# Norms with the rounded part first, four weight tiles walked together, and low parts made by VectorE

## The reference

```python
for i in range(DEPTH):                       # DEPTH = 4, kind = i % 3
    mp = mixer(xp)                           # hgrn2, dsa or s5
    xp = layer_norm(DN_ALPHA * xp + mp, ln_mix_g[i], ln_mix_b[i])
    xp = layer_norm(DN_ALPHA * xp + sq_relu_mlp(xp, mlp_w1[i], mlp_w2[i]), ln_ffn_g[i], ln_ffn_b[i])

def layer_norm(x, g, b):
    mu = jnp.mean(xf, -1, keepdims=True)
    var = jnp.mean(jnp.square(xf - mu), -1, keepdims=True)
    return ((xf - mu) * lax.rsqrt(var + LN_EPS) * g + b)
```

## Time and profile before

| what | us |
|---|---|
| timed runs, median (lowest to highest) | 3243.29 (3243.13 to 3245.08) |
| profiled execution, its own time | 3235.7 |
| profiled execution, span from first to last instruction | 3233.9 |
| TensorE busy in the span | 2885.5 |
| VectorE, ScalarE, GpSimd busy | 1479.6, 1051.1, 1042.7 |
| mean granted TensorE clock (share of full) | 0.923 |

### The profile page before, as it was taken

The page is one execution under the profiler, slowest core; times in us unless marked ns, Lnnn a source line. Parts: engine busy times, 40 slices in busy tenths (PEclk is TensorE's granted clock), DMA queues, the critical chain, the costliest instruction groups (busy, mean ns, idle before and its releaser), DMA issues. The chain is left out here.

```text
span 3233.9 us, 54787 instructions
## 1 busy us (share of the span) xinstructions
PE 2885.5 (89%) x22296; PEld 2787.9 (86%) x22296; DVE 1479.6 (46%) x2170; ACT 1051.1 (33%) x1612; POOL 1042.7 (32%) x548
## 2 busy tenths in 40 slices
PE   7999789999899998999943777999989998899997
PEld 7999789999769998999942677999989997799997
DVE  4555363251327425506249844713425554461442
ACT  4554432222331434212241223312235554331222
POOL 2000453445523126344430025534440001453442
PEclk9999899999897979999976579999999998899999
DMA  4222122222334322222231012222223221122221
GB/s 138 81 81 80 55 72 85 91 84 85 104 84 164 123 69 78 85 91 91 85 95 23 23 50 79 85 85 91 85 72 100 90 81 56 60 86 83 91 85 65
DMA packets 118301, 267.52 MB, mean 83 GB/s; under 512 B 10274, under 2 KB 57890, under 8 KB 118018
## 3 DMA queue, kind: packets, MB, share of 16 engines
q1 hardware_dynamic: 56592, 206.10, 19.2%
q10 hardware_dynamic: 56434, 41.41, 4.8%
q0 software_dynamic: 5120, 17.83, 1.5%
HBM read 242.24 MB, written 23.07 MB: 82 GB/s over the span
## 5 line engine op out<-in xcount | busy, mean ns | idle before, releaser
L1515 PE MATMUL lp<-xh,wh 128*128 128x260 f32 x4176 | 1225.3, 293 | 129.3 <-POOL xl L398 118.8
L1517 PE MATMUL lp<-xh,wl 128*128 128x260 f32 x4176 | 1202.2, 288 | 0.0
L1516 PE MATMUL lp<-xl,wh 128*128 128x260 f32 x4176 | 1200.6, 287 | 0.0
L388 POOL TENSOR_TENSOR wl<-raw,wh 128x1024 fp32r<-128x1024 f32 x325 | 800.8, 2465 | 934.0 <-ACT wh L525 612.7
L1515 PEld LDWEIGHTS lp<-xh,wh 128*128 128x128 f32 x4176 | 812.3, 195 | 158.3 <-issue 121.8
L1516 PEld LDWEIGHTS lp<-xl,wh 128*128 128x128 f32 x4176 | 811.5, 194 | 0.5
L1517 PEld LDWEIGHTS lp<-xh,wl 128*128 128x128 f32 x4176 | 810.3, 194 | 0.0
L1515 PE MATMUL lp<-hh,wh 128*128 128x260 f32 x2048 | 588.3, 287 | 40.9 <-DVE hl L1489 40.9
L1517 PE MATMUL lp<-hh,wl 128*128 128x260 f32 x2048 | 586.4, 286 | 0.0
L1516 PE MATMUL lp<-hl,wh 128*128 128x260 f32 x2048 | 584.7, 285 | 0.0
L1515 PEld LDWEIGHTS lp<-hh,wh 128*128 128x128 f32 x2048 | 394.3, 193 | 42.5 <-POOL wl L388 42.5
(11 more groups left out here) (327 smaller groups left out, 2970.8 us busy)
## 6 DMA issues: line engine op xcount, KB each, us to landing
raw<-in_wstream SPq DMA_DIRECT2D x389, 512.0 KB, 3.5
s<-in_s_in ACTq DMA_DIRECT2D x16, 512.0 KB, 5.7
out_hg_s<-s ACTq DMA_DIRECT2D x16, 512.0 KB, 3.3
pg<-in_kpages POOLq DMA_DIRECT2D x16, 512.0 KB, 5.1
pg<-in_vpages POOLq DMA_DIRECT2D x16, 512.0 KB, 5.6
bias_rows<-bsm ACTq DMA_DIRECT2D x1, 2560.0 KB
x<-in_xT ACTq DMA_DIRECT2D x4, 520.0 KB, 7.6
out_kT<-r ACTq DMA_DIRECT2D x1, 2080.0 KB, 6.7
```

The costliest lines, as they stand in the source:

```text
L388: pool.tensor_tensor(wl[:, s, :], raw[:, r_, :], wh[:, s, :].bitcast(F32), ALU.subtract).then_inc(w_low, 1)
L1515: pe.matmul(bank(T, half), wh[:, slot, w], hi[:, k0 + k, t], start=first, stop=False)
L1516: pe.matmul(bank(T, half), wh[:, slot, w], lo[:, k0 + k, t], start=False, stop=False)
L1517: ins = pe.matmul(bank(T, half), wl[:, slot, w], hi[:, k0 + k, t], start=False, stop=last)
```

## The change

Three things. First, in a norm ACT squares the mean straight out of PSUM, VectorE's first operation is the variance, the gain is applied by VectorE (`scalar_tensor_tensor`), ACT makes `xh` from VectorE's row before `x`, and VectorE makes `xl` one block behind (`low_part`); four rows of `lw` are used in turn. POOL makes no `xl` for these norms. Second, `pair` becomes `lead`: for block k it waits for `xh` only and does wh·xh and wl·xh, and the wh·xl products follow one block later. Third, `four` walks four tiles together at the start of the HGRN, DSA and MLP stages, the third and fourth into `mb`, and finishes them one by one at the last two blocks; DSA's fifth tile comes before the indexer key's statistics.

```diff
+    def out_banks(T, in_mb=False):
+        return (mb if in_mb else lp)[:, 2 * (T % 2):2 * (T % 2) + 2, 0:NH2]
+    NORM_ROWS = (6, 7, 2, 3)
...
@@ gpsimd
-            split(x, 8 * (3 * y["i"] + 2))
...
-            if y["i"] < L - 1:
-                split(x, 8 * (3 * y["i"] + 3))
...
@@ scalar: finish_norm
             act.preload_act_table_set("natural_log_exp_and_others")
+            act.wait_ge(stats_ready, ln + 1)
+            act.activation(halves(lw[:, 6, :]), mb[:, 0:2, 0:NH2], ACT.Square).then_inc(msq_ready, 1)
             act.wait_ge(var_ready, ln + 1)
...
                 act.wait_ge(norm_ready, 8 * ln + m + 1)
-                act.activation(x[:, m, :], lw[:, 6 + m % 2, :], ACT.Identity, scale=lnp[:, kind, y["i"], m:m + 1],
-                               bias=lnp[:, kind + 1, y["i"], m:m + 1]).then_inc(x_ready, 1)
+                row, shift = lw[:, NORM_ROWS[m % 4], :], lnp[:, kind + 1, y["i"], m:m + 1]
                 if not last:
-                    act.wait_ge(x_ready, 8 * ln + m + 1)
-                    act.activation(xh[:, m, :], x[:, m, :], ACT.Copy).then_inc(xh_ready, 1)
+                    act.activation(xh[:, m, :], row, ACT.Identity, bias=shift).then_inc(xh_ready, 1)
+                act.activation(x[:, m, :], row, ACT.Identity, bias=shift).then_inc(x_ready, 1)
...
@@ vector: norm
             dve.wait_ge(stats_ready, ln + 1)
+            dve.wait_ge(msq_ready, ln + 1)
+            dve.tensor_tensor(halves(rstd), mb[:, 2:4, 0:NH2], halves(lw[:, 6, :]), ALU.subtract).then_inc(var_ready, 1)
             link.step(dve.tensor_copy(halves(mean), mb[:, 0:2, 0:NH2]))
-            link.step(dve.tensor_tensor(lw[:, 6, :], mean, mean, ALU.mult))
-            dve.tensor_tensor(halves(rstd), mb[:, 2:4, 0:NH2], halves(lw[:, 6, :]), ALU.subtract).then_inc(var_ready, 1)
+            def low_part(m):
+                n0 = 8 * (3 * y["i"] + 2 + ln % 2)
+                dve.wait_ge(xh_ready, n0 + m + 1)
+                dve.wait_ge(x_ready, 8 * ln + m + 1)
+                dve.tensor_tensor(xl[:, m, :], x[:, m, :], xh[:, m, :].bitcast(F32), ALU.subtract).then_inc(xl_dve, 1)
...
-                link.step(dve.tensor_tensor(lw[:, 6 + m % 2, :], r[:, m, :], mean, ALU.subtract))
+                if m >= 4:
+                    dve.wait_ge(x_ready, 8 * ln + m - 3)
+                link.step(dve.tensor_tensor(row, r[:, m, :], mean, ALU.subtract))
                 if m == 0:
                     dve.wait_ge(rstd_ready, ln + 1)
-                dve.tensor_tensor(lw[:, 6 + m % 2, :], lw[:, 6 + m % 2, :], rstd, ALU.mult).then_inc(norm_ready, 1)
+                dve.scalar_tensor_tensor(row, row, gain, rstd, ALU.mult, ALU.mult).then_inc(norm_ready, 1)
+                if m and not final:
+                    low_part(m - 1)
...
@@ tensor
+        def piece(n, T, k, low_, in_mb, last):
+            w, slot = slice(k * P, (k + 1) * P), n % SPL
+            for half in range(2):
+                t, out = slice(half * NH2, (half + 1) * NH2), out_banks(T, in_mb)[:, half, :]
+                if low_:
+                    ins = pe.matmul(out, wh[:, slot, w], xl[:, k, t], start=False, stop=last and k == KT - 1)
+                else:
+                    pe.matmul(out, wh[:, slot, w], xh[:, k, t], start=k == 0, stop=False)
+                    ins = pe.matmul(out, wl[:, slot, w], xh[:, k, t], start=False, stop=False)
+            return ins
...
+        def lead(tiles, split, ks):
+            ks = list(ks)
+            for at, k in enumerate(ks + [None]):
+                if k is not None:
+                    pe.wait_ge(xh_ready, split + k + 1)
+                    for n, T, in_mb in tiles:
+                        if k == 0:
+                            pe.wait_ge(*low_count(n))
+                            if T >= 2 and not in_mb:
+                                pe.wait_ge(tile_out, T - 1)
+                        piece(n, T, k, False, in_mb, False)
+                if at:
+                    pe.wait_ge(*low_part_count(split + ks[at - 1]))
+                    for n, T, in_mb in tiles:
+                        ins = piece(n, T, ks[at - 1], True, in_mb, True)
+                        if ks[at - 1] == KT - 1:
+                            ins.then_inc(chunk_done, 1)
...
         def pair(n, T, split, ks=range(KT)):
-            for k in ks:
-                part(n, T, (k,), split)
-                part(n + 1, T + 1, (k,), split)
+            lead([(n, T, False), (n + 1, T + 1, False)], split, ks)
+        def four(n, T, split):
+            tiles = [(n + a, T + a, a >= 2) for a in range(4)]
+            lead(tiles, split, range(KT - 2))
+            for one in tiles:
+                lead([one], split, range(KT - 2, KT))
...
-                    pair(c1, t1, 8 * (3 * y["i"] + 2))
-                    s0_ = 1
+                    four(c1, t1, 8 * (3 * y["i"] + 2))
```

More of the change, by code:

```diff
@@ L392, in low_at, with split @@
                 low(n, n % SPL, n % RAW)
-        def split(src, n0, ms=range(KT)):
+        def split(src, n0, ms=range(KT), made=None):
             for m in ms:
                 pool.wait_ge(xh_ready, n0 + m + 1)
+                if made is not None:
+                    pool.wait_ge(x_ready, made + m + 1)
                 pool.tensor_tensor(xl[:, m, :], src[:, m, :], xh[:, m, :].bitcast(F32), ALU.subtract
@@ L604, in copy_out @@
                     p, T = h % 2, t0 + 4 * h + j
-                    src = lp[:, 2 * (T % 2):2 * (T % 2) + 2, 0:NH2]
+                    src = out_banks(T, h == 0 and j >= 2)
                     act.wait_ge(chunk_done, c0 + 4 * h + j + 1)
@@ L706, in copy_tile @@
                     T = t0 + c
-                    act.activation(halves(dst), lp[:, 2 * (T % 2):2 * (T % 2) + 2, 0:NH2], ACT.Copy, **kw
+                    act.activation(halves(dst), out_banks(T, 2 <= c < 4), ACT.Copy, **kw
                                    ).then_inc(tile_out, 1)
@@ L728, in _ @@
                     copy_tile(c, qi[:, c - 1, :])
-                    if c == 1:
+                    if c == 4:
                         act.wait_ge(ki_var, 1)
@@ L989, in _ @@
                 act.wait_ge(tile_out, t1)
+                first = 0
                 def hidden(i):
@@ L998, in hidden @@
                             act.wait_ge(h_ready, i * 4 + (g1 + c - 1))
-                        act.activation(halves(lw[:, 6 + c % 2, :]), lp[:, 2 * (T % 2):2 * (T % 2) + 2, 0:NH2], ACT.Relu
+                        act.activation(halves(lw[:, 6 + c % 2, :]), out_banks(T, half == 0 and i is first and c >= 2), ACT.Relu
                                        ).then_inc(tile_out, 1)
-                hidden(0)
+                hidden(first)
                 with act.Fori(1, HHALF // 4) as i:
@@ L1618, in dsa @@
         def dsa(y, c0, t0):
-            pair(c0, t0, 8 * 3 * y["i"])
+            four(c0, t0, 8 * 3 * y["i"])
+            tile(c0 + 4, t0 + 4)
             pe.wait_ge(ki_raw, 1)
+            pe.wait_ge(tile_out, t0 + 4)
             pe.wait_ge(b_loaded, 16 * 8)
@@ L1627, in dsa @@
             ins.then_inc(ki_stats, 1)
-            for c in range(2, 5):
-                tile(c0 + c, t0 + c)
             pe.wait_ge(ki_var, 1)
@@ L1820, in _ @@
                     if h == 0:
-                        pair(c0, t0, 8 * 3 * y["i"])
-                        for j in range(2, 4):
-                            tile(c0 + j, t0 + j)
+                        four(c0, t0, 8 * 3 * y["i"])
                     else:
@@ L1916, in _ @@
                 c1, t1 = y["cm"] + 32 * half, y["tm"] + 24 * half
-                s0_ = 0
                 if half == 0:
-                    pair(c1, t1, 8 * (3 * y["i"] + 2))
-                    s0_ = 1
+                    four(c1, t1, 8 * (3 * y["i"] + 2))
                 g1 = HHALF * (2 * y["i"] + half)
                 if half == 0:
-                    for c in range(2, 4):
-                        tile(c1 + c, t1 + c)
                     lo_, hi_ = 1, HHALF // 4
```

16 lines of the change are left out of this document (13 added, 3 removed).

## The result

The changed kernel takes 3327.59 us (median of four runs, 3317.54 to 3345.29) against 3244.18 us (3243.13 to 3258.04) for the one before: a ratio of 1.0253, 95% interval 1.0193 to 1.0313. The forecast was 3315, range 3266 to 3358, slower: the sign came out as forecast, and the time lies in the range, 12.6 us above the forecast. The profiled execution took 3337.49 us against 3235.7.

The account below looks back on a forecast made before the run. The matrix engine, busy 89% of 3233.9 us, was taken as the bound; 83.4 us lost less 11.8 given back, net 71.6, made 3235.7 profiled into 3307, and 7.6 more for the timed median gave 3315, range 3266 to 3358.

Parts of the forecast that it names:

- The deciding step: At seven starts PE does 12 matmuls, then stands until the norm is through on ACT and the fourth tile split.
- Steps (1) to (6): MLP norm, first multiply to four tiles' end: 46.4 us instead of 36.6, plus 1.5 behind; 11.3 us lost each.
- Layer 1: Layer 1's start: late fourth split, then fifth tile and uncovered indexer statistics; 877.6 against 863.9, 13.7 us lost.
- The start and layer 3: Kernel start and layer 3: VectorE's late fourth split, with 1.6 us behind it, loses 11.9 and 12.6 us.
- Given back: Gains: 3.0 us at the S5 layer, 0.8 at the last norm, 8.0 in `pair`; together 11.8 us.
- the tails of `pair`: Output products: PE starts with xh while POOL still makes xl; twice per HGRN layer, once in layers 1 and 2; 8.0 us.
- Slower still: Norms: VectorE's low parts at the contended price, 6 us a norm, giving 3355; chance 0.12.
- Less slow: Starts: full clock on return, ACT-bound rounds, no wait behind the four tiles; 42 us less, 3273; chance 0.13.
- Faster: Starts: the fourth split does not hold PE; seven starts win 45 us, the rest 12, giving 3186; chance 0.04.

Follow-up runs that it names:

- fix: Changed kernel with the fourth tile's split made ahead of the norm, four tiles still walked together; 3223.61 us, ratio 0.9929 to the kernel before.
- three: Changed kernel with three tiles walked together and the fourth alone behind them, no split moved; 3198.76 us, ratio 0.9857 to the kernel before.
- again: The changed kernel run once more with no edit; 3325.47 us, ratio 1.0251 to the kernel before.

## Why the prediction was right, point by point

**The deciding step.** "The fourth tile's wait stands in front of everything that four tiles could do during the norm" is shown, by the seven waits and by `fix` and `three`, which end the wait from its two sides. At each of the six norms with a walk behind it ACT starts `wh` after the last `x`, 0.62 us after it at the four MLPs. The Trainium skill (PSUM — Partial Sum Buffer, section "Engine vs sequencer instructions") calls ScalarE's queue a strict FIFO; the trace agrees.

**Two readings of the kernel before.** The forecast put all 21 waits for `xl` at the norms; 60.5 of the 118.8 us lie there. And the fourth tile is needed there after one pair and one tile, not two pairs. Neither number enters the sum.

**Steps (1) to (6) at an MLP norm.** At layer 3's: first multiply 3.02 us after the statistics (forecast 3.02), a round of 2.02 (1.97; the multiply with gain takes 0.76 where 0.69 was taken), the last `x` at 18.1 (18.0), PE on again at 22.24 (22.2), four tiles ended at 46.5 (46.4), a wait of 1.27 behind them (1.5). A stage lost 9.7 to 10.9 us, where 11.3 were forecast: 42.2 for 45.2.

**Layer 1.** PE went on 25.9 us after the statistics, behind a wait of 18.3, as these waits of the changed kernel show:

```profile
PE mb L1563 <- POOL wl L394: 18.3, 1, 18.3
...
PE mb L1702 <- DVE lw L1222: 3.5, 1, 3.5
```

The second is the indexer's statistics without their cover: 3.5 us for 2.2, since VectorE's square took 1.95 beside POOL. The indexer's matmuls came 14.1 us later (forecast 13.7). The stage lost 17.9 where 12.4 were forecast net of the tail. The next 3.2 us lie in those matmuls, 48 small ones of the indexer (L1702; before 863.68 to 870.79, then 901.61 to 911.94). They took 7.11 us at a granted 0.74 and take 10.33 at 0.50, behind the wait of 3.5:

```profile
863.68:870.79 7.11, 7.11 (x50) 7.09 (x48) 0.00 (x0) 0.60 (x1) 5.88 (x8) 0.74 0.63 191
901.61:911.94 10.33, 10.33 (x48) 10.31 (x48) 3.08 (x3) 2.16 (x3) 5.17 (x7) 0.50 0.49 162
```

Up to the tail the delay grows to 21.3 us, and the tail, from its first `xh` to the end of the statistics, is 3.4 shorter (51.3 for 54.7).

**The start and layer 3.** Four tiles end at 55.87 at the start (forecast 55.5). The first gate of VectorE behind the norm came 14.5 us later in layer 0 and 14.1 in layer 3, where 11.9 and 12.6 were forecast: copies and loads behind the fourth tile come late as well. That is the right mechanism with a term too small by 1.5 to 2.6 us.

**Given back.** Layer 2 gained 1.6 us for the forecast's 4.1, the end 0.4 for 0.8. Of the 8.0 us at the tails of `pair`, 5.6 were to come from the HGRN layers, and most of them did not. PE's waits there for `xl`, now for `xh`, did fall, from 40.4 us to 31.7 in all layers, though three waits of 0.4 to 0.6 us for PSUM stand behind them that were not there before. But from the first `xh` of the tail to the end of the statistics an HGRN layer takes 76.9 and 77.0 us before, 76.5 in layer 0 of the changed kernel and 76.8 in both layers of `again`: 0 to 0.4 back for 2.8. In layer 3 of the changed kernel it takes 75.0, as in the other profiles with the new `pair` whose last head takes 45.8 us. Starting earlier on `xh` let PE wait less there, and not end earlier by as much.

**What was missed.** The forecast for the profiled execution was +71.6; it was +101.9, and +94.9 in `again`. Of the 30 us between, layer 3 holds 21.0, layer 1 5.5, layer 0 3.8, layer 2 2.5, and the MLP stages give back 3.0. Layer 3's 30.8 are 14.1 up to the first gate and 18.8 in its heads (from the first gate to the last 301.7 us against 282.8), less 2.1 at the tail. `again` has the same 14.1, and 3.1 in the heads: with the same program its layer 3 is 14.0 us shorter. So more than half of this miss is the pace of the heads (last section), a term that the prediction did not have. Without the heads of layers 0 and 3 it is some 13 us: the tails, layer 1, layer 2 and the starts, less what the MLP stages gave back. By medians the miss is 12 us (83.4 for 71.6). The forecast had no term for the heads, so that they seem to weigh little in the medians was luck.

**The rivals.** "Slower still" fell: VectorE's low parts took 0.69 to 0.70 us with POOL idle. The Trainium skill (SBUF — State Buffer, section "SBUF: two separate sides") says that a VectorE operation with two SBUF inputs and a GpSimd operation that reads SBUF exclude each other on a shared pair of ports; the 0.70 us alone and the 1.95 us of the square beside POOL agree. "Less slow" had the right price for the half clock (2.7; measured 2.6) and the wrong guess that it would not be paid. "Faster" was priced at 3186 for a split made early; `fix` gave 3224. Its four tiles ended at 30.6 us after the statistics, as priced (30.2), and its MLP stages gained 4.2 to 6.1 each, 21 in all. What did not come are the gains elsewhere: in the profiled execution layer 1 gained 2.3, but layers 0, 2 and 3 lost 12.7, 3.2 and 4.1. In layer 0 these are 4.7 up to the first gate and 9.8 in the heads, less 1.8 at the tail, in layer 2 the wait for the weight load; in layer 3 the start gained 3.1 and the heads lost 7.7.

## What to carry to other kernels

Before a walk over several tiles is widened, look where the preparation of the last of them stands on its engine: if it is queued behind the very work that the walk is to run beside, the first step of the walk waits for all of it. Widen to what is ready by then and no further: three tiles, with the fourth walked alone behind them, gained 1.4% where four lost 2.5%. A wait at the first step holds all that is queued behind it on the waiting engine, so put waits as late in the walk as the data allow. And preparing a tile earlier than it is needed can hold what stands behind it: at one norm the early split cost 4 us, because its weights had not yet been loaded.

## What the runs showed of the hardware

The same loop body ran at three paces. Most heads of the HGRN layers (314 matmuls seen in each) take close to 39.5, 41.1 or 45.8 us, all three in one execution, and PE waits no more than 0.3 us at a time in the two shown. They are neighbours of layer 3 in the changed kernel; the third row is the slow stretch in the second:

```profile
2568.30:2607.80 39.50, 39.09 (x314) 37.14 (x313) 22.50 (x42) 20.77 (x37) 0.00 (x0) 1.00 0.27 83
2607.80:2653.60 45.80, 45.38 (x314) 42.93 (x313) 22.46 (x42) 20.74 (x37) 0.00 (x0) 0.85 0.23 71
2633.60:2648.80 15.20, 15.20 (x63) 13.39 (x62) 1.92 (x2) 2.70 (x4) 0.00 (x0) 0.55 0.09 33
```

VectorE and ACT do the same work in both; only the granted clock differs, 1.00 against 0.85. In the second it fell to the half level (1.2 GHz) at 2634.7, in the middle of matmuls: PE had been busy for 25.38 of the 25.8 us before that stretch, at a granted 1.00, and was busy through all 15.20 us of it. The heads of the changed kernel's layer 3 alternate, 45.8, 39.5, 45.8, 39.5; in `again` one is 45.8 and four are 39.5. The profile of the kernel before has no head above 41.1. The runs of one program differ by up to 33 us (3316.24 to 3348.93 in `again`), and the two profiles of it differ by 15.8 us in the heads of layer 3, so a single profile can't judge a smaller change in these layers. Why a head falls to one pace or the other was not settled; no kernel here tried to set it.
